# A mixture-of-experts stage with 96 instead of 128 slots for an expert, and up to three sweeps over the experts instead of two

## The chip, the core and the metric

The program runs on one NeuronCore of a Trainium2 chip. The core has five engines with programs of their own: TensorE (PE; matmuls, and PEld for its loads of the stationary operand), VectorE (DVE), ScalarE (ACT), GpSimd (POOL) and SyncE (SP), which issues most transfers. They wait for one another by semaphores. The metric is the device time of one execution in microseconds; of three runs of the kernel before, the median is 1677.79 us (1676.78 to 1679.43).

## The reference, cut to what matters

The trunk takes 256 frames of width 1024 through a retention layer with a dense SwiGLU, then a stick-breaking attention layer with a mixture of experts. All of it is float32. The change touches the last part alone:

```python
def moe_swiglu(h, router, w_in, w_out):
    hf = h.reshape(B * S, D)                       # 256 x 1024
    logits = (hf @ router).astype(jnp.float32)     # 8 experts
    top_v, top_i = lax.top_k(logits, TOP_K)        # 2 experts for each frame
    top_w = jax.nn.softmax(top_v, axis=-1)
    gates = jnp.sum(jax.nn.one_hot(top_i, N_EXPERTS) * top_w[..., None], axis=1)
    for e in range(N_EXPERTS):
        y = y + gates[:, e:e + 1] * swiglu(hf, w_in[e], w_out[e])
    # swiglu: a, b = split(h @ w_in); (silu(a) * b) @ w_out; w_in 1024 x 7168, w_out 3584 x 1024
```

256 frames with two choices each give 512 assignments for 8 experts, 64 on average.

## The kernel before, in words

**Precision.** A product of two float32 matrices is made from three passes (`passes`, L490 to L494): both operands are split into a high part, rounded to the type fp32r, and a low part, the rest; then high times high (L492), activations high times weights low (L493), and activations low times weights high (L494). The stationary operand (first argument) holds the activations, the moving one (second) 512 columns of weights.

**Weights.** They come in chunks of 1 MB into a ring of 6 raw slots, loaded by SP (L259, L270). A chunk is split in two quarters of 1024 columns each: ACT writes the high part (`w_hi`, L964), DVE the low part (`w_lo`, L1302), into rings of 3 slots. PE waits for DVE (`lo_done`), ACT waits for PE to free a slot (`w_used`), and SP waits for DVE to free a raw slot.

**Experts.** The router's choices become, for each expert, a list of slots: the first chosen frame takes slot 0, the next slot 1, and so on. `one_hot` (L1661) writes a matrix of frames by slots. `gather` (L869) multiplies it with the frames, so that an expert's frames stand in its slots; ACT copies the result (`ht`, L1230), PE transposes it in 8 blocks (`transpose_gathered`, L883), ACT and DVE split it in high and low (`hg_hi` L1234, `hg_lo` L1686). Then 7 tiles of 512 hidden columns follow. For one tile PE makes `up` twice (a and b, 24 matmuls each), ACT the silu (L1222), DVE the product with b (`e_g`, L1677), PE 4 transposes of it (`transpose_product`, L866), ACT and DVE its high and low part (`eT_hi` L1226, `eT_lo` L1681), and PE `down` (24 matmuls). `down` of a tile stands behind `up` of the next one on PE, so the split of its operand has a tile's time. `scatter` (L899, L900) brings the slots back to the frames, and DVE adds them with the gates (L1705). In a transpose the data is the stationary operand and the identity the moving one.

**Sweeps.** If the fullest expert has more frames than slots, the whole stage runs again for the frames left over (L1668: `npass` is 1 or 2), with the weights loaded again. Every engine reads `npass` and loops over it.

Of the kernel before, what the change touches and what calls it, by code (L numbers as in the profile page):

```python
# [16 lines left out]
P = 128  # L17
S = 256
D = 1024
NB = S // P  # L20
# [6 lines left out]
FW = 256  # L27
FT = FF // FW
NE, FE = 8, 3584
ET = FE // TW  # L30
EPS = 1e-6
RAW, RING = 6, 3
# [20 lines left out]
def trunk(nc, x_d, c_d, pos_d, ada_w, ada_b, norm_mix, norm_ff, ret_w_in, ret_gn, ret_w_out, kv_ada_w,  # L53
# [7 lines left out]
    with ctx:  # L61
# [105 lines left out]
            return buf.rearrange("p h (t q) -> p h t q", q=P)[:, :, 0:3:2, :]  # L167


        y32 = fa(0, D)  # L170
        e_sa = fa(2048, TW)
        e_g = fa(2560, TW)
        ht = fa(5120, D)
        hk_hi = hT_hi[:, :, :].rearrange("p c s -> p (c s)").rearrange("p (b d) -> p b d", b=NB)
        hk_lo = hT_lo[:, :, :].rearrange("p c s -> p (c s)").rearrange("p (b d) -> p b d", b=NB)
        hg_hi = ra(0, KC, P)
        hg_lo = ra(1024, KC, P)
        eT_hi = ra(2048, 4, P)
        eT_lo = ra(2560, 4, P)
        hot = ra(3072, NB, P)  # L180
        hotT = ra(3328, S)
        y_hi = ra(3584, D)
        y_lo = ra(4608, D)
# [55 lines left out]
        def _(sp):  # L239
# [249 lines left out]
        def _(pe):  # L489
# [367 lines left out]
            def down(c, m, n, first, last_one):  # L857

                pe.wait_ge(eTl_ok, n + 1)
                for h in range(2):  # L860
                    by_rows(c + h, m, eT_hi, eT_lo, 2 * h, 1, 4, first and h == 0, last_one and h == 1)

            def transpose_product(n):
                pe.wait_ge(eg_ok, n + 1)
                for c in range(4):
                    last = pe.transpose(ps[:, 2, c * P:(c + 1) * P], e_g[:, c * P:(c + 1) * P], ident[:, :])  # L866
                last.then_inc(eT_done, 1)

            def gather(ne):  # L869

                pe.wait_ge(hot_ok, ne + 1)
                for n in range(2):
                    cols = slice(n * TW, (n + 1) * TW)
                    for b in range(NB):
                        pe.matmul(ps[:, 6 + n, :], hot[:, b, :], hk_hi[:, b, cols], start=b == 0, stop=False)  # L875
                        last = pe.matmul(ps[:, 6 + n, :], hot[:, b, :], hk_lo[:, b, cols], start=False,  # L876
                                         stop=b == NB - 1)
                last.then_inc(ga_done, 1)

            def transpose_gathered(ne):  # L880
                pe.wait_ge(ht_ok, ne + 1)
                for c in range(KC):
                    last = pe.transpose(ps[:, 6 + c // 4, (c % 4) * P:(c % 4 + 1) * P], ht[:, c * P:(c + 1) * P],  # L883
                                        ident[:, :])
                last.then_inc(hgT_done, 1)

            def transpose_hot():
                for b in range(NB):
                    last = pe.transpose(ps[:, 3, b * P:(b + 1) * P], hot[:, b, :].bitcast(f32), ident[:, :])
                last.then_inc(hotT_done, 1)  # L890

            def scatter(ne):
# [29 lines left out]
            pe.wait_ge(hk_ok, 1)  # L922
            gather(0)
            pe.wait_ge(npass_ok, 1)
            npass = pe.value_load(npass_t[0:1, 0:1], min_val=1, max_val=2)
            with pe.Fori(0, npass) as p:
                m0 = NE * ET * p
                with pe.If(p):
# [23 lines left out]
        def _(act):  # L952
# [266 lines left out]
            def tile_silu(n, c, m):  # L1219

                act.wait_ge(w_used, before_half(c, m))
                act.activation(e_sa, ps[:, 0, :], ACT.Silu).then_inc(esa_ok, 1)  # L1222

            def tile_high(n):
                act.wait_ge(eT_done, n + 1)
                act.activation(eT_hi.rearrange("p c s -> p (c s)"), ps[:, 2, :], ACT.Copy).then_inc(eTh_ok, 1)  # L1226

            def gathered_out(ne):
                act.wait_ge(ga_done, ne + 1)
                act.activation(ht.rearrange("p (n q) -> p n q", n=2), ps[:, 6:8, :], ACT.Copy).then_inc(ht_ok, 1)  # L1230

            def gathered_high(ne):
                act.wait_ge(hgT_done, ne + 1)
                act.activation(hg_hi.rearrange("p (n c) s -> p n (c s)", n=2), ps[:, 6:8, :], ACT.Copy)\  # L1234
                   .then_inc(hgh_ok, 1)

            def y_high(ne):
# [3 lines left out]
            def step(j, me, ne, more=True):  # L1241

                c, n = U_MOE + 4 + RAW * (j - 1), me + j
                split_quarters(c, me, 5, 9)
                act.wait_ge(eg_ok, n)
                tile_silu(n, c + 2, me)
                split_quarters(c, me, 9, 12)
                if j < ET - 1 or more:
                    split_quarters(c, me, 12, 14)
                    if j == ET - 1:  # L1250
                        gathered_high(ne + 1)
                    split_quarters(c, me, 14, 17)
                tile_high(n)
                if j == ET:
                    y_high(ne)
                if j == 2:
                    act.wait_ge(hotT_done, ne + 1)
                    act.activation(hotT, ps[:, 3, 0:S], ACT.Copy).then_inc(hotT_ok, 1)
# [4 lines left out]
            npass = act.value_load(npass_t[0:1, 0:1], min_val=1, max_val=2)  # L1263
            with act.Fori(0, npass) as p:
                m0 = NE * ET * p
                with act.If(p):
# [26 lines left out]
        def _(dve):  # L1293
# [364 lines left out]
            def one_hot(ne, e):  # L1658

                for b in range(NB):  # L1660
                    ins = v.tensor_scalar(hot[:, b, :], slot_no[:, :], slot[:, b, ds(e, 1)], sel[:, b, ds(e, 1)],  # L1661
                                          ALU.is_equal, ALU.mult)
# [10 lines left out]
            def tile_product(n, c, m):  # L1673

                dve.wait_ge(esa_ok, n + 1)
                dve.wait_ge(w_used, before_half(c, m))
                v.tensor_tensor(e_g, ps[:, 1, :], e_sa, ALU.mult).then_inc(eg_ok, 1)  # L1677

            def tile_low(n):
                dve.wait_ge(eTh_ok, n + 1)  # L1680
                v.tensor_tensor(eT_lo.rearrange("p c s -> p (c s)"), ps[:, 2, :],  # L1681
                                eT_hi.rearrange("p c s -> p (c s)").bitcast(f32), ALU.subtract).then_inc(eTl_ok, 1)

            def gathered_low(ne):
                dve.wait_ge(hgh_ok, ne + 1)
                v.tensor_tensor(hg_lo.rearrange("p (n c) s -> p n (c s)", n=2), ps[:, 6:8, :],  # L1686
                                hg_hi.rearrange("p (n c) s -> p n (c s)", n=2).bitcast(f32),
                                ALU.subtract).then_inc(hgl_ok, 1)

            def y_gated(ne, c, m):  # L1690

                dve.wait_ge(w_used, before_half(c, m))
                v.tensor_tensor(y32.rearrange("p (n q) -> p n q", n=2), ps[:, 4:6, :],
                                gate_f[:, :].rearrange("p (n q) -> p n q", n=2), ALU.mult).then_inc(yg_ok, 1)

            def y_low(ne):
                dve.wait_ge(yh_ok, ne + 1)
# [33 lines left out]
                    one_hot(ne + 1, e + 1)  # L1731

            dve.wait_ge(npass_ok, 1)
            npass = dve.value_load(npass_t[0:1, 0:1], min_val=1, max_val=2)
            dve.wait_ge(gbc_ev, 4)
            with dve.Fori(0, npass) as p:
                steps.enter(p, 1)
# [92 lines left out]
```

## Time and profile before

| | |
|---|---|
| median of three runs | 1677.79 us |
| profiled execution, first to last instruction | 1675.8 us, 22,428 instructions |
| PE busy | 1565.9 us (93%), 7164 matmuls |
| PEld busy | 1294.4 us (77%) |
| DVE busy | 1405.6 us (84%) |
| ACT busy | 1085.8 us (65%) |
| HBM read | 499.28 MB, 299 GB/s over the span |
| granted TensorE clock | 0.968 of 2.4 GHz on average |

The page gives no time of the profiled execution but its span; the median of the runs lies 2.0 us above it. The stage of the experts goes from about 668 us to about 1667 us. A PE that is busy all the time is not a PE at its peak: matmuls overlap, each is recorded as some 0.39 us long, while they start 0.23 us apart.

### The profile page before, as it was taken

What the parts mean: (1) busy time and instruction counts of PE and PEld (TensorE: products, weight loads), DVE (VectorE), ACT (ScalarE), POOL (GpSimd) and SP (SyncE); (2) the same over time, 40 slices, a digit from 0 to 9 for tenths busy, and PEclk for the clock granted to TensorE, in tenths of its full rate; (3) what the DMA queues carried; (4) which work ended last, traced back from release to release, by engine and by line L of the source; (5) the groups of instructions that cost most, each with busy time, mean ns of one, the idle gap of its engine ahead of it and who ended that gap; (6) DMA issues with size and microseconds to landing.
All of it is one profiled execution on the core that took longest, in us unless ns stands there. A gap on an engine that the chain in (4) does not pass through costs nothing.

```text
span 1675.8 us, 22428 instructions
## 1 busy us (share of the span) xinstructions
PE 1565.9 (93%) x7164; PEld 1294.4 (77%) x7164; DVE 1405.6 (84%) x1537; ACT 1085.8 (65%) x1176; POOL 58.1 (3%) x47
## 2 busy tenths in 40 slices
PE   4999997999979676899999999999999999999996
PEld 4788775888768555788888888888888888888884
DVE  6889997788876444698998998998998998998995
ACT  3444434444454653687787777787787787787874
POOL 0212200000000120000000000000000000000000
PEclk9999998999989787899999999999999999999998
DMA  9977785888848102599999999999999999999991
GB/s 335 349 246 278 265 274 199 276 300 314 294 171 274 50 3 75 212 392 356 349 375 355 348 381 352 350 380 344 364 372 343 358 384 343 358 377 345 353 383 79
DMA packets 235113, 500.89 MB, mean 299 GB/s; under 512 B 9744, under 2 KB 40640, under 8 KB 235072
## 3 DMA queue, kind: packets, MB, share of 16 engines
q1 hardware_dynamic: 233904, 500.29, 82.6%
q8 instruction: 24, 0.39, 0.1%
q10 hardware_dynamic: 1168, 0.07, 0.0%
q14 instruction: 17, 0.14, 0.0%
HBM read 499.28 MB, written 1.05 MB: 299 GB/s over the span
## 4 chain that ended last, share of the span: by engine, by line
PE 81%; DVE 9%; DMA 3%; issue 3%; ACT 3%; POOL 1%; DVEq 0%; SPq 0%; ACTq 0%; POOLq 0%
PE ps L492 24%; PE ps L494 24%; PE ps L493 24%; DVE acc L1321 2%; DVE w_lo L1302 2%; DMA ada<-in_ada_w 2%; PE ps L866 1%; PE ps L767 1%; DMA raw<-in_ret_w_in 1%; PE ps L525 1%; DMA ada<-in_kv_ada_w 1%; PE ps L899 1%; PE ps L875 1%; PE ps L876 0%; PE ps L900 0%
## 5 line engine op out<-in xcount | busy, mean ns | idle before, releaser
L1302 DVE TENSOR_TENSOR w_lo<-raw,w_hi 128x1024 fp32r<-128x1024 f32 x834 | 990.9, 1225 | 100.2 <-ACT w_hi L964 86.2
L964 ACT ACTIVATE w_hi<-raw 128x1024 fp32r<-128x1024 f32 x834 | 864.5, 1058 | 246.3 <-PE ps L494 229.4
L492 PE MATMUL ps<-w_hi,RA 128*128 128x512 f32 x1560 | 618.1, 396 | 9.0 <-DVE w_lo L1302 2.9
L494 PE MATMUL ps<-w_hi,RA 128*128 128x512 f32 x1560 | 609.4, 391 | 0.0
L493 PE MATMUL ps<-w_lo,RA 128*128 128x512 f32 x1560 | 608.4, 390 | 0.0
L492 PEld LDWEIGHTS ps<-w_hi,RA 128*128 128x128 f32 x1560 | 293.7, 188 | 68.7 <-issue 3.4
L494 PEld LDWEIGHTS ps<-w_hi,RA 128*128 128x128 f32 x1560 | 293.4, 188 | 62.4
L493 PEld LDWEIGHTS ps<-w_lo,RA 128*128 128x128 f32 x1560 | 294.0, 188 | 59.4 <-issue 0.7
L492 PE MATMUL ps<-w_hi,hT_hi 128*128 128x512 f32 x432 | 172.6, 399 | 8.1 <-DVE hT_lo L1372 6.9
L494 PE MATMUL ps<-w_hi,hT_lo 128*128 128x512 f32 x432 | 170.2, 394 | 0.0
L493 PE MATMUL ps<-w_lo,hT_hi 128*128 128x512 f32 x432 | 170.1, 394 | 0.0
L1321 DVE SCALAR_TENSOR_TENSOR acc<-ada,cond,acc 128x512 f32<-128x512 f32 x189 | 150.6, 797 | 2.5
L492 PEld LDWEIGHTS ps<-w_hi,hT_hi 128*128 128x128 f32 x432 | 82.6, 191 | 25.7 <-DVE hT_lo L1372 7.7
L494 PEld LDWEIGHTS ps<-w_hi,hT_lo 128*128 128x128 f32 x432 | 82.2, 190 | 17.7
L493 PEld LDWEIGHTS ps<-w_lo,hT_hi 128*128 128x128 f32 x432 | 82.5, 191 | 16.6
L1226 ACT ACTIVATE RA<-ps 128x512 fp32r<-128x512 f32 x56 | 33.6, 600 | 61.6 <-PE ps L866 61.6
L1681 DVE TENSOR_TENSOR RA<-ps,RA 128x512 fp32r<-128x512 f32 x56 | 38.6, 689 | 22.8 <-ACT RA L1226 19.2
L1318 DVE TENSOR_SCALAR acc<-ada,cond 128x512 f32<-128x512 f32 x27 | 13.1, 484 | 36.9 <-DMA ada<-in_ada_w 34.5
L1222 ACT ACTIVATE FA<-ps 128x512 f32<-128x512 f32 x56 | 33.4, 596 | 13.8 <-PE ps L494 13.8
L1677 DVE TENSOR_TENSOR FA<-ps,FA 128x512 f32<-128x512 f32 x56 | 38.4, 685 | 3.1 <-PE ps L494 3.1
L525 PE MATMUL ps<-ident,FA 128*128 128x128 f32 x64 | 14.6, 422 | 27.6 <-DVE FA L1354 27.6
L1103 ACT ACTIVATE FA<-ps 128x512 f32<-128x512 f32 x11 | 6.6, 600 | 47.3 <-PE ps L494 47.3
(220 smaller groups left out, 874.0 us busy)
## 6 DMA issues: line engine op xcount, KB each, us to landing
raw<-in_moe_w_in SPq DMA_DIRECT2D x224, 1024.0 KB
raw<-in_moe_w_out SPq DMA_DIRECT2D x112, 1024.0 KB
ada<-in_ada_w SPq DMA_DIRECT2D x46, 1024.0 KB, 7.3
raw<-in_ff_w_in SPq DMA_DIRECT2D x44, 512.0 KB
raw<-in_ret_w_in SPq DMA_DIRECT2D x16, 1024.0 KB
raw<-in_ff_w_out SPq DMA_DIRECT2D x11, 1024.0 KB
raw<-in_ret_w_in SPq DMA_DIRECT2D x16, 512.0 KB
raw<-in_ret_w_out SPq DMA_DIRECT2D x8, 1024.0 KB
```

The source lines that it names most:

```text
L492: pe.matmul(out, a_hi, b_hi, start=first, stop=False)
L493: pe.matmul(out, a_hi, b_lo, start=False, stop=False)
L494: return pe.matmul(out, a_lo, b_hi, start=False, stop=last)
L525: last = pe.transpose(ps[:, c // 2, (c % 2) * S + b * P:(c % 2) * S + (b + 1) * P], (xn0 if n == 0 else xn)[:, b, c * P:(c + 1) * P], iden ...
L767: pe.matmul(o[:, 0:S], after[:, :], lm[:, h, 0:S], start=True, stop=False)
L964: act.activation(w_hi[:, cn % RING, cols], raw[:, cn % RAW, cols], ACT.Copy).then_inc(hi_done, 1)
L1222: act.activation(e_sa, ps[:, 0, :], ACT.Silu).then_inc(esa_ok, 1)
L1226: act.activation(eT_hi.rearrange("p c s -> p (c s)"), ps[:, 2, :], ACT.Copy).then_inc(eTh_ok, 1)
L1302: v.tensor_tensor(w_lo[:, cn % RING, cols], raw[:, cn % RAW, cols], w_hi[:, cn % RING, cols].bitcast(f32), ALU.subtract).then_inc(lo_done, 1)
L1321: ins = v.scalar_tensor_tensor(a, ada[:, h, cols], cond[:, kc:kc + 1], a, ALU.mult, ALU.add)
L1677: v.tensor_tensor(e_g, ps[:, 1, :], e_sa, ALU.mult).then_inc(eg_ok, 1)
L1681: v.tensor_tensor(eT_lo.rearrange("p c s -> p (c s)"), ps[:, 2, :], eT_hi.rearrange("p c s -> p (c s)").bitcast(f32), ALU.subtract).then_i ...
```

## The change

An expert gets `CAP = 96` slots. Everything with one column or one row for a slot shrinks with it: the one-hot matrix, the gathered frames, their transposes, the stationary operands of `up` and `down`, the transposes of the product, and the high and low parts of all these. Results of `up`, `down` and `gather` take 96 partitions in place of 128; their moving operand stays 512 columns wide. Tiles that have the slots on their partitions (`y32`, `e_sa`, `e_g`, `ht`, `hotT`, `y_hi`, `y_lo`) keep their row length. `down` has its own loop now, with the same order as `by_rows`. `npass` can be 1, 2 or 3, and takes one more DVE instruction; SP loops over the sweeps behind the first.

```diff
+CAP, SWEEPS = 96, 3
-        hg_hi = ra(0, KC, P)
+        hg_hi = ra(0, KC, CAP)
-        eT_hi = ra(2048, 4, P)
+        eT_hi = ra(2048, 4, CAP)
-            npass = sp.value_load(npass_t[0:1, 0:1], min_val=1, max_val=2)
+            npass = sp.value_load(npass_t[0:1, 0:1], min_val=1, max_val=SWEEPS)
             with sp.If(npass - 1):
-                experts(NE * ET)
+                with sp.Fori(1, npass) as p:
+                    experts(NE * ET * p)
-                        last = passes(ps[:, bank, :], hg_hi[:, kc, :], hg_lo[:, kc, :], w_hi[:, s, cols],
+                        last = passes(ps[0:CAP, bank, :], hg_hi[:, kc, :], hg_lo[:, kc, :], w_hi[:, s, cols],
...
-                    last = pe.transpose(ps[:, 2, c * P:(c + 1) * P], e_g[:, c * P:(c + 1) * P], ident[:, :])
+                    last = pe.transpose(ps[:, 2, c * CAP:(c + 1) * CAP], e_g[:, c * P:(c + 1) * P],
+                                        ident[0:CAP, 0:CAP])
...
-                    last = pe.transpose(ps[:, 6 + c // 4, (c % 4) * P:(c % 4 + 1) * P], ht[:, c * P:(c + 1) * P],
-                                        ident[:, :])
+                    last = pe.transpose(ps[:, 6 + c // 4, (c % 4) * CAP:(c % 4 + 1) * CAP], ht[:, c * P:(c + 1) * P],
+                                        ident[0:CAP, 0:CAP])
...
-                act.activation(eT_hi.rearrange("p c s -> p (c s)"), ps[:, 2, :], ACT.Copy).then_inc(eTh_ok, 1)
+                act.activation(eT_hi.rearrange("p c s -> p (c s)"), ps[:, 2, 0:4 * CAP], ACT.Copy).then_inc(eTh_ok, 1)
...
-            v.tensor_scalar(npass_t[:, :], stat[:, 16:17], float(P), 1.0, ALU.is_gt, ALU.add).then_inc(npass_ok, 1)
+            steps.link(v.tensor_scalar(stat[:, 20:21], stat[:, 16:17], float(CAP), 1.0, ALU.is_gt, ALU.add))
+            v.scalar_tensor_tensor(npass_t[:, :], stat[:, 16:17], float(2 * CAP), stat[:, 20:21], ALU.is_gt,
+                                   ALU.add).then_inc(npass_ok, 1)
...
-                v.tensor_tensor(eT_lo.rearrange("p c s -> p (c s)"), ps[:, 2, :],
+                v.tensor_tensor(eT_lo.rearrange("p c s -> p (c s)"), ps[:, 2, 0:4 * CAP],
...
-                steps.link(v.tensor_scalar(slot, slot, -float(P), None, ALU.add))
+                steps.link(v.tensor_scalar(slot, slot, -float(CAP), None, ALU.add))
```

No instruction changes its place; the forms change. On PE, at the end of a tile, before (partitions of the result by columns of the moving operand; `ident` with `FA` is a transpose, `w_hi` and `w_lo` with `RA` are the passes of `up` and `down`):

```order
L492 MATMUL ps<-w_hi,RA 128x512
L493 MATMUL ps<-w_lo,RA 128x512
L494 MATMUL ps<-w_hi,RA 128x512
L864 REGISTER_ALU
L866 MATMUL ps<-ident,FA 128x128 x4
L498 REGISTER_ALU
L492 MATMUL ps<-w_hi,RA 128x512
```

And the same place in the changed kernel:

```order
L494 MATMUL ps<-w_hi,RA 96x512
L495 MATMUL ps<-w_lo,RA 96x512
L496 MATMUL ps<-w_hi,RA 96x512
L874 REGISTER_ALU
L876 MATMUL ps<-ident,FA 128x96 x4
L500 REGISTER_ALU
L494 MATMUL ps<-w_hi,RA 96x512
```

The passes keep their 512 columns and write 96 partitions; the four transposes keep 128 partitions and have 96 columns. On DVE, ahead of the first tile, in the changed kernel (the slots, the one-hot matrix of the first expert, the count of the fullest expert and the number of sweeps):

```order
L1676 COPY FA<-ps 128x16
L1672 TENSOR_SCALAR RA<-slot_no,FA 128x96 x2
L1678 TENSOR_REDUCE stat<-ps 128x1
L1679 TENSOR_SCALAR stat<-stat 128x1
L1680 SCALAR_TENSOR_TENSOR npass_t<-stat 128x1
```

One instruction on 128x1 is added, L1679.

## Rows read from the trace of the kernel before

**Rows 1.** The page's 40 slices: granted TensorE clock, in tenths
```profile
PEclk9999998999989787899999999999999999999998
```

**Rows 2.** Stretches: length; PE, PEld, DVE, ACT, POOL busy us (count); clock, DMA share, GB/s
```profile
1109.63:1126.43 16.80, 16.80 (x79) 13.91 (x77) 15.45 (x15) 13.50 (x14) 0.00 (x0) 1.00 1.03 380
...
700.00:1640.00 940.00, 940.00 (x4285) 778.35 (x4284) 869.92 (x807) 747.05 (x785) 0.00 (x0) 1.00 0.99 362
```

**Rows 3.** Waits, 700 to 1640 us: total us, times, longest
```profile
ACT w_hi L964 <- PE ps L494: 119.8, 403, 0.7
ACT RA L1226 <- PE ps L866: 52.4, 54, 2.5
```

**Rows 4.** Groups by form, 700 to 1640 us: busy us, mean ns, idle before
```profile
L1302 DVE TENSOR_TENSOR w_lo<-raw,w_hi 128x1024 fp32r<-128x1024 f32 x650 | 765.5, 1221 | 49.1 <-ACT w_hi L964 35.8
...
L1681 DVE TENSOR_TENSOR RA<-ps,RA 128x512 fp32r<-128x512 f32 x54 | 37.2, 689 | 17.0 <-ACT RA L1226 13.4
...
L1226 ACT ACTIVATE RA<-ps 128x512 fp32r<-128x512 f32 x54 | 32.4, 600 | 52.4 <-PE ps L866 52.4
```

**Rows 5.** Timeline around one set of four transposes: start us, us long
```profile
1109.25 0.58 PEld L866 LDWEIGHTS ps<-ident,FA 128*128 128x128 f32 x4
1109.47 0.60 PE L866 MATMUL ps<-ident,FA 128*128 128x128 f32 x4
...
1109.80 0.19 PEld L492 LDWEIGHTS ps<-w_hi,RA 128*128 128x128 f32 x1
...
1109.91 0.19 PEld L493 LDWEIGHTS ps<-w_lo,RA 128*128 128x128 f32 x1
...
1110.14 0.39 PE L493 MATMUL ps<-w_lo,RA 128*128 128x512 f32 x1
```

**Rows 6.** Chain of waits, 1100 to 1140 us: start us, us on the chain
```profile
1109.63 0.44 PE ps L866 x4
...
1126.43 0.44 PE ps L866 x4
```

**Rows 7.** All transposes of the product, then of the gathered frames: ns min/median/max
```profile
L866 PE MATMUL ps<-ident,FA x224: 270/272/327, 691.5 to 1649.8; 128*128 128x128 f32 x112
...
L883 PE MATMUL ps<-ident,FA x64: 270/272/331, 673.4 to 1524.2; 128*128 128x128 f32 x64
```

**Rows 8.** Timeline of PEld alone: the first transpose load, then the first two merged
```profile
673.37 0.14 PEld L883 LDWEIGHTS ps<-ident,FA 128*128 128x128 f32 x1 [1.83 <-ACT FA L1230]
...
673.37 0.20 PEld L883 LDWEIGHTS ps<-ident,FA 128*128 128x128 f32 x2 [1.83 <-ACT FA L1230]
```

**Rows 9.** Timeline of PE in the retention layer: float32 without a split
```profile
120.52 0.60 PE L631 MATMUL ps<-FA 128*128 128x256 f32 x2
120.96 0.38 PE L632 MATMUL ps<-FA 128*128 128x128 f32 x2
121.18 0.60 PE L631 MATMUL ps<-FA 128*128 128x256 f32 x2
```

**Rows 10.** Timeline ahead of the first tile
```profile
667.76 0.60 DVE L1661 TENSOR_SCALAR RA<-slot_no,FA 128x128 fp32r<-128x128 f32 x2
...
673.37 1.09 PE L883 MATMUL ps<-ident,FA 128*128 128x128 f32 x8 [1.11 <-ACT FA L1230]
674.50 1.02 ACT L1234 ACTIVATE RA<-ps 128x1024 fp32r<-128x1024 f32 x1 [1.19 <-PE ps L883]
675.56 1.23 DVE L1686 TENSOR_TENSOR RA<-ps,RA 128x1024 fp32r<-128x1024 f32 x1 [4.67 <-ACT RA L1234]
...
676.93 0.79 PE L492 MATMUL ps<-w_hi,RA 128*128 128x512 f32 x1 [2.46 <-DVE RA L1686]
```

**Rows 11.** Timeline at the last tile
```profile
1650.08 0.60 ACT L1226 ACTIVATE RA<-ps 128x512 fp32r<-128x512 f32 x1 [7.54 <-PE ps L866]
1650.58 3.89 ACT L964 ACTIVATE w_hi<-raw 128x1024 fp32r<-128x1024 f32 x4
```

**Rows 12.** A load of 64 stationary columns in the attention, by form
```profile
L781 PEld LDWEIGHTS ps<-FA 128*64 128x64 f32 x16 | 1.2, 137 | 0.5
```

More of the change, by code:

```diff
@@ L167, in on_diagonal @@
             return buf.rearrange("p h (t q) -> p h t q", q=P)[:, :, 0:3:2, :]
[L170 to L173, printed above, removed]
+        y32 = fa(0, D)[0:CAP]
+        e_sa = fa(2048, TW)[0:CAP]
+        e_g = fa(2560, TW)[0:CAP]
+        ht = fa(5120, D)[0:CAP]
         hk_hi = hT_hi[:, :, :].rearrange("p c s -> p (c s)").rearrange("p (b d) -> p b d", b=NB)
         hk_lo = hT_lo[:, :, :].rearrange("p c s -> p (c s)").rearrange("p (b d) -> p b d", b=NB)
-        hg_hi = ra(0, KC, P)
-        hg_lo = ra(1024, KC, P)
-        eT_hi = ra(2048, 4, P)
[L179 to L183, printed above, removed]
+        hg_hi = ra(0, KC, CAP)
+        hg_lo = ra(1024, KC, CAP)
+        eT_hi = ra(2048, 4, CAP)
+        eT_lo = ra(2560, 4, CAP)
+        hot = ra(3072, NB, CAP)
+        hotT = ra(3328, S)[0:CAP]
+        y_hi = ra(3584, D)[0:CAP]
+        y_lo = ra(4608, D)[0:CAP]
         logit, gate_e, sel, slot, oh1, oh2, mx = (fa(3072 + 16 * n, NB, NE) for n in range(7))
@@ L860, in down @@
                 for h in range(2):
-                    by_rows(c + h, m, eT_hi, eT_lo, 2 * h, 1, 4, first and h == 0, last_one and h == 1)
+                    s = (c + h) % RING
+                    for t in range(2):
+                        landed(c + h, m, t)
+                        for k in range(2):
+                            cols = slice(t * D + k * TW, t * D + (k + 1) * TW)
+                            last = passes(ps[0:CAP, 4 + k, :], eT_hi[:, 2 * h + t, :], eT_lo[:, 2 * h + t, :],
+                                          w_hi[:, s, cols], w_lo[:, s, cols], first and h == 0 and t == 0,
+                                          last_one and h == 1 and t == 1)
+                        last.then_inc(w_used, 1)
             def transpose_product(n):
@@ L874, in gather @@
                     for b in range(NB):
-                        pe.matmul(ps[:, 6 + n, :], hot[:, b, :], hk_hi[:, b, cols], start=b == 0, stop=False)
-                        last = pe.matmul(ps[:, 6 + n, :], hot[:, b, :], hk_lo[:, b, cols], start=False,
+                        pe.matmul(ps[0:CAP, 6 + n, :], hot[:, b, :], hk_hi[:, b, cols], start=b == 0, stop=False)
+                        last = pe.matmul(ps[0:CAP, 6 + n, :], hot[:, b, :], hk_lo[:, b, cols], start=False,
                                          stop=b == NB - 1)
@@ L888, in transpose_hot @@
                 for b in range(NB):
-                    last = pe.transpose(ps[:, 3, b * P:(b + 1) * P], hot[:, b, :].bitcast(f32), ident[:, :])
+                    last = pe.transpose(ps[0:CAP, 3, b * P:(b + 1) * P], hot[:, b, :].bitcast(f32), ident[:, :])
                 last.then_inc(hotT_done, 1)
@@ L924, in _ @@
             pe.wait_ge(npass_ok, 1)
-            npass = pe.value_load(npass_t[0:1, 0:1], min_val=1, max_val=2)
+            npass = pe.value_load(npass_t[0:1, 0:1], min_val=1, max_val=SWEEPS)
             with pe.Fori(0, npass) as p:
@@ L1221, in tile_silu @@
                 act.wait_ge(w_used, before_half(c, m))
-                act.activation(e_sa, ps[:, 0, :], ACT.Silu).then_inc(esa_ok, 1)
+                act.activation(e_sa, ps[0:CAP, 0, :], ACT.Silu).then_inc(esa_ok, 1)
             def tile_high(n):
                 act.wait_ge(eT_done, n + 1)
-                act.activation(eT_hi.rearrange("p c s -> p (c s)"), ps[:, 2, :], ACT.Copy).then_inc(eTh_ok, 1)
+                act.activation(eT_hi.rearrange("p c s -> p (c s)"), ps[:, 2, 0:4 * CAP], ACT.Copy).then_inc(eTh_ok, 1)
             def gathered_out(ne):
                 act.wait_ge(ga_done, ne + 1)
-                act.activation(ht.rearrange("p (n q) -> p n q", n=2), ps[:, 6:8, :], ACT.Copy).then_inc(ht_ok, 1)
+                act.activation(ht.rearrange("p (n q) -> p n q", n=2), ps[0:CAP, 6:8, :], ACT.Copy).then_inc(ht_ok, 1)
             def gathered_high(ne):
                 act.wait_ge(hgT_done, ne + 1)
-                act.activation(hg_hi.rearrange("p (n c) s -> p n (c s)", n=2), ps[:, 6:8, :], ACT.Copy)\
+                act.activation(hg_hi.rearrange("p (n c) s -> p n (c s)", n=2), ps[:, 6:8, 0:4 * CAP], ACT.Copy)\
                    .then_inc(hgh_ok, 1)
@@ L1257, in step @@
                     act.wait_ge(hotT_done, ne + 1)
-                    act.activation(hotT, ps[:, 3, 0:S], ACT.Copy).then_inc(hotT_ok, 1)
+                    act.activation(hotT, ps[0:CAP, 3, 0:S], ACT.Copy).then_inc(hotT_ok, 1)
                 if j == ET - 2 and more:
@@ L1262, in _ @@
             act.wait_ge(npass_ok, 1)
-            npass = act.value_load(npass_t[0:1, 0:1], min_val=1, max_val=2)
+            npass = act.value_load(npass_t[0:1, 0:1], min_val=1, max_val=SWEEPS)
             with act.Fori(0, npass) as p:
@@ L1660, in one_hot @@
                 for b in range(NB):
-                    ins = v.tensor_scalar(hot[:, b, :], slot_no[:, :], slot[:, b, ds(e, 1)], sel[:, b, ds(e, 1)],
+                    ins = v.tensor_scalar(hot[:, b, :], slot_no[:, 0:CAP], slot[:, b, ds(e, 1)], sel[:, b, ds(e, 1)],
                                           ALU.is_equal, ALU.mult)
@@ L1676, in tile_product @@
                 dve.wait_ge(w_used, before_half(c, m))
-                v.tensor_tensor(e_g, ps[:, 1, :], e_sa, ALU.mult).then_inc(eg_ok, 1)
+                v.tensor_tensor(e_g, ps[0:CAP, 1, :], e_sa, ALU.mult).then_inc(eg_ok, 1)
             def tile_low(n):
                 dve.wait_ge(eTh_ok, n + 1)
-                v.tensor_tensor(eT_lo.rearrange("p c s -> p (c s)"), ps[:, 2, :],
+                v.tensor_tensor(eT_lo.rearrange("p c s -> p (c s)"), ps[:, 2, 0:4 * CAP],
                                 eT_hi.rearrange("p c s -> p (c s)").bitcast(f32), ALU.subtract).then_inc(eTl_ok, 1)
@@ L1685, in gathered_low @@
                 dve.wait_ge(hgh_ok, ne + 1)
-                v.tensor_tensor(hg_lo.rearrange("p (n c) s -> p n (c s)", n=2), ps[:, 6:8, :],
+                v.tensor_tensor(hg_lo.rearrange("p (n c) s -> p n (c s)", n=2), ps[:, 6:8, 0:4 * CAP],
                                 hg_hi.rearrange("p (n c) s -> p n (c s)", n=2).bitcast(f32),
@@ L1692, in y_gated @@
                 dve.wait_ge(w_used, before_half(c, m))
-                v.tensor_tensor(y32.rearrange("p (n q) -> p n q", n=2), ps[:, 4:6, :],
-                                gate_f[:, :].rearrange("p (n q) -> p n q", n=2), ALU.mult).then_inc(yg_ok, 1)
+                v.tensor_tensor(y32.rearrange("p (n q) -> p n q", n=2), ps[0:CAP, 4:6, :],
+                                gate_f[0:CAP, :].rearrange("p (n q) -> p n q", n=2), ALU.mult).then_inc(yg_ok, 1)
             def y_low(ne):
@@ L1733, in _ @@
             dve.wait_ge(npass_ok, 1)
-            npass = dve.value_load(npass_t[0:1, 0:1], min_val=1, max_val=2)
+            npass = dve.value_load(npass_t[0:1, 0:1], min_val=1, max_val=SWEEPS)
             dve.wait_ge(gbc_ev, 4)
```

## The prediction

> **What bounds the kernel now.** I read the page's slices first, then the stretch of the experts' tiles alone, its waits, and last the timeline of one tile's end. The slices show where the time lies: from slice 17 on, nearly all of it is the experts [rows 1]. In 940 us of that stretch PE is busy for 940.00 us at the full clock (1.00, that is 2.4 GHz); DVE is busy for 869.92 us (93%), ACT for 747.05 us, and the transfers take 0.99 of their engines at 362 GB/s [rows 2]. The waits say who is late: ACT's long sum of waiting is for PE, 119.8 us for a free weight slot and 52.4 us for the transposes [rows 3]. DVE's idle time before `w_lo` ends mostly by ACT [rows 4], which itself waits for PE. Nobody on PE waits for a weight, so PE's own instructions set the end here, and a change is worth what it takes off PE, as long as DVE (7% to spare) and the transfers keep up.
>
> One tile takes 1126.43 - 1109.63 = 16.80 us, of which the four transposes stand on the chain with 0.44 us [rows 6]. The other 72 matmuls share 16.36 us: 0.227 us each.
>
> **The 72 matmuls of a tile.** Their number and their 512 moving columns stay. What shrinks is the load of the stationary operand, 128 columns to 96. That load is covered: the next one follows a load after 0.11 us where nothing else holds it (1109.80 to 1109.91), while matmuls are 0.227 us apart [rows 5]. So I take nothing for it. The price bounds are these: 512 columns at 2.4 GHz are 0.213 us, so 0.014 us of each spacing is not streaming; if the load caused all of it and 96 columns removed it, 4032 + 64 of `gather` = 4096 matmuls would give 57 us. If a quarter went with a quarter of the columns, 14 us. The nearest row is the float32 matmul without a split: 256 columns, each held twice as long, with the same load of 128 columns, two of them in 120.96 - 120.52 = 0.44 us, 0.22 us each [rows 9]. There the load costs nearly nothing beyond streaming, so the excess seems to belong to how fp32r streams, and I stay at zero.
>
> **The transposes.** Here the moving operand is the identity, and it goes from 128 to 96 columns, while the stationary operand keeps 128. Which of the two sets their spacing? Four take 0.44 us, 0.109 us each [rows 6]. The float32 matmuls of 128 columns take the same: two in 121.18 - 120.96 = 0.22 us, and doubling the columns doubles the time [rows 9], so this spacing looks like 128 columns at two array clocks each (0.107 us). The load of a transpose is shorter: the first is 0.14 us long and the first two together 0.20 us, so the second began 0.06 us behind the first [rows 8], against 0.11 us between the loads for the passes. With 0.06 us of load under 0.107 us of streaming, the streaming sets the pace, and 96 columns take 0.080 us: 0.0267 us less for each.
>
> The Trainium skill, "TensorE: Matmul & The Clock Gate", section LDWEIGHTS, says the contrary for this case: a load costs its columns divided by 1.2 GHz, whatever the rows, and 128 columns would be 107 ns, just what is measured between transposes; the 128 columns stay, so by it nothing is gained. The 0.06 us between two such loads [rows 8] speaks against it. It is a rival below.
>
> Counts: 224 transposes of the product and 64 of gathered frames [rows 7], 288 in all; 288 x 0.0267 = 7.7 us. All 224 lie on PE's full stretch; of the 64, 8 are ahead of the first tile on the chain too [rows 10]. Each set's last transpose gives its share only if the load for the following pass, 0.11 us now [rows 5], shrinks with its columns. The load of 64 columns is 137 ns long [rows 12] against 0.19 us for 128 [rows 5], so it does; if it didn't, 64 sets would lose 1.7 us. I take 7.7 us.
>
> The two transposes of the one-hot matrix keep 128 moving columns; `scatter` keeps its 512 moving and 128 stationary columns: nothing.
>
> **Ahead of the first tile** the steps are one behind the other [rows 10]. ACT's copy costs 0.80 ns a column (1.02 us here for 1024, 0.600 for 512 [rows 4]): 256 columns less are 0.21 us. DVE's is 1.23 us here for 1024 and 0.689 for 512 [rows 4], 1.05 ns a column: 0.27 us. The one-hot matrix, two times 32 columns less: about 0.05 us. The added DVE instruction for the number of sweeps stands behind `one_hot`, which frees `gather`; PE's `gather` and ACT's copy of its result follow until the transposes start at 673.37 [rows 10], so it is hidden; without that cover it would be about 0.2 us (one small link of that chain). Sum 0.5 us. The clock changes level in this place (digits 7 and 8 in slices 15 and 16, counted from 0 [rows 1]), and a start 0.5 us earlier can shift one such level by a step; I allow 2 us for that either way.
>
> **In the tiles** ACT's `eT_hi` gets 128 x 0.80 = 0.10 us shorter and DVE's `eT_lo` 128 x 1.05 = 0.13 us; the hidden side of a pair, so they give only slack: DVE falls by 7 us of 870. **At the last tile** PE has no `up` to cover it: ACT starts `w_hi` only behind `eT_hi` [rows 11], so 0.10 us comes off the end.
>
> Register instructions and loop overhead on SP and PE stay as they are in the one sweep that runs. That only one runs follows from the reference itself: worked through on its own inputs, the fullest expert has 77 of the 512 assignments, and 76 to 86 with five other random draws. Transfers: the same bytes in 7.7 us less need 0.8% more than 362 GB/s; the tile looked at above ran at 380 GB/s [rows 2], so they follow.
>
> **Sum.** 7.7 + 0.5 + 0.1 = 8.3 us off the span of 1675.8 us, that is 1667.5 us. The median of the runs shown lies 2.0 us above the span, so 1677.8 - 8.3 = 1669.5 us.
>
> **The rivals.**
> - *The loads set the transposes' pace* (the 128 stationary columns stay). For it: the number 0.107 fits as well, and PEld is busy at the transposes without a gap [rows 5]. Against: the 0.06 us of [rows 8]. Then only 0.6 us is gained: 1677.2 us. The transfers could have the same outcome if the 0.99 share [rows 2] were a real ceiling, but then PE should wait for weights now and then.
> - *The passes get faster too.* For it: 0.014 us over streaming in each. Against: [rows 9]. By a quarter: 1669.5 - 14 = 1655.5 us. In full: 1669.5 - 57 = 1612 us on paper, but DVE has 7% and the transfers little more, so rather 1625 us.
> - *The load of 96 columns turns slow* and is no longer covered: the side that ends slower. The place is every pass; it decides only when a load takes over 0.227 us where it now takes 0.11. At four times the present rate for each column, 0.75 x 0.44 = 0.33 us, the spacing becomes 0.33 and 4096 x 0.10 = 420 us are added: about 2090 us. For it speaks no row; against it, the 64-column load of 137 ns [rows 12], which shows no cliff off the full width. The Trainium skill, same page, section on the weight-path modes, has a rule of this kind: fast loading needs exactly 128 weights and a type other than FP32. If the passes used it, 96 columns would lose it. Their load is no faster than one of plain float32 in this trace, so I see nothing to lose.
> - *A second sweep runs after all* (an expert with over 96 frames). It would double the stretch from 673 to 1667 us: some 2670 us. Only if the routing on the chip were far from the reference's.
>
> **How the numbers follow.** Transposes faster, passes unchanged: 60%, with its own range 1665 to 1675 us. Transposes unchanged or the gain lost to transfers: 17%. Passes faster as well: 18%, 10 of it for the small form. Loads slow: 4%. Second sweep: 1%. The predicted time is the first one's, 1669.5 us. The range takes in the second and the small form of the third and leaves out the rest: 1653 to 1679 us. What can be told from no change is about 0.2%, 3.4 us. Faster by more than that: the third case and nearly all of the first (8.3 us is well over 3.4, the shift of the clock may eat it in one of fifteen): 0.74. The same: the second case and the rest of the first: 0.20. Slower: 0.06, with a little for what I have not thought of.
>
> **What would show it.** Right: in the profile after, a set of four transposes on the chain takes about 0.33 us in place of 0.44, a tile 16.69 in place of 16.80 us, with PE still busy throughout and passes 0.227 us apart. The transposes' step is wrong if the set stays at 0.44. The step on the passes is wrong if their spacing falls below 0.225 or rises, and the cover is wrong if PE begins to wait for `w_lo`. A count of 7164 matmuls confirms one sweep.

## The result, and the profile after

The changed kernel takes 1687.0 us in the median of 5 runs (1686.36 to 1689.1), the kernel before 1679.43 us (5 runs, 1676.78 to 1682.88) beside it. The ratio is 1.0052 with a 95% interval of 1.0041 to 1.0063: 8.7 us slower by the ratio, 7.6 us by the two medians. Forecast were 8.3 us less, and a range of 1653 to 1679 us.

The profiled execution has a span of 1687.4 us, the slowest of its five runs (1684.6 to 1687.4). It has the same 7164 matmuls and HBM read the same 499.28 MB: one sweep ran. The stretch of the experts, in the columns of [rows 2], with one tile first:

```profile
1114.55:1131.60 17.05, 17.05 (x80) 11.97 (x78) 15.40 (x15) 13.44 (x14) 0.00 (x0) 1.00 1.01 376
...
700.00:1640.00 940.00, 940.00 (x4241) 661.97 (x4240) 855.34 (x799) 734.25 (x776) 0.00 (x0) 1.00 0.98 358
```

PE is still busy all the time at the full clock, so it is still what sets the end, and it gets through 4241 matmuls in 940 us where it was 4285. Every other engine has less to do: PEld 662 us against 778, DVE 855 against 870, ACT 734 against 747. The chain of waits around two sets of transposes, as in [rows 6]:

```profile
1114.56 0.33 PE ps L876 x4
1131.57 0.33 PE ps L876 x4
```

A set takes 0.33 us and not 0.44, as forecast. But the tile takes 1131.57 - 1114.56 = 17.01 us and not 16.80 [rows 6], so the 72 passes share 16.68 us: 0.2317 us each, where they had 0.2272. The timeline at that set answers to [rows 5]:

```profile
1114.17 0.39 PE L496 MATMUL ps<-w_hi,RA 128*96 128x512 f32 x1
1114.17 0.54 PEld L876 LDWEIGHTS ps<-ident,FA 96*128 96x128 f32 x4
...
1114.40 0.49 PE L876 MATMUL ps<-ident,FA 96*128 96x96 f32 x4
1114.65 0.16 PEld L494 LDWEIGHTS ps<-w_hi,RA 128*96 128x96 f32 x1
...
1114.73 0.17 PEld L495 LDWEIGHTS ps<-w_lo,RA 128*96 128x96 f32 x1
```

The load got shorter, 0.16 us where it was 0.19, and the next one follows after 0.08 us and not 0.11. It is covered with room to spare, and still the pass beside it became slower. Groups of the same stretch, the columns of [rows 4]:

```profile
L494 PE MATMUL ps<-w_hi,RA 128*96 128x512 f32 x1281 | 508.1, 397 | 0.0
L496 PE MATMUL ps<-w_hi,RA 128*96 128x512 f32 x1282 | 506.1, 395 | 0.0
...
L1694 DVE TENSOR_TENSOR RA<-ps,RA 128x384 fp32r<-128x384 f32 x53 | 29.4, 554 | 12.4 <-ACT RA L1237 12.4
...
L1237 ACT ACTIVATE RA<-ps 128x384 fp32r<-128x384 f32 x53 | 26.1, 493 | 47.9 <-PE ps L876 47.9
```

DVE's and ACT's part of the product got shorter as worked out (689 to 554 ns, 600 to 493 ns). PE waits for nobody at its passes (0.0).

The starts of successive passes show how the pace differs. Before, 89% of them are 226 or 227 ns, one behind the other; only the first nine behind a set of transposes are uneven (227 to 235 ns on average, single ones up to 236), and then the even step is found again. After, the passes of `up` and `down` never find it: of all steps 0.3% are 226 or 227 ns, 13% are at most 228, nearly half are over 231 and 16% are 236 or more. The mean between 700 and 1640 us (steps under 240 ns) is 227.2 ns before and 231.6 ns after.

**The account.** 4160 passes of the stage (4032 of `up` and `down`, 64 of `gather`, 64 of `scatter`) x 4.34 ns = 18.1 us more; transposes 7.7 us less; the short copies 0.6 us less: 9.8 us. The runs say 8.7 us (0.52%, 6.9 to 10.6 us). In the profiled executions the part from the first pass of `up` to the last set of transposes went from 972.5 to 981.3 us, 8.8 us, but the clock had a share in it: at its start PE ran at a granted clock of 0.50 (1.2 GHz) for 5.47 us before, and the same length was granted 0.73 on average after. The rows, in the columns of [rows 2], before and then after:

```profile
676.93:682.40 5.47, 5.47 (x13) 4.36 (x14) 1.23 (x1) 1.06 (x1) 0.00 (x0) 0.50 0.00 0
...
678.66:684.13 5.47, 5.47 (x18) 3.82 (x19) 1.23 (x1) 2.13 (x3) 0.00 (x0) 0.73 0.00 0
```

(0.73 - 0.50) x 5.47 = 1.3 us of full-speed work came free, so at one clock that part would have lost about 10.1 us; its share of the account is 10.6 us, because the copies and the first expert's transposes lie ahead of it. The spans of the two profiled executions differ by 11.6 us. Of this, 2.5 us arise ahead of the experts, where the code is the same, 0.8 us are won back ahead of the first tile, and 1.1 us come behind the last set of transposes, where the clock was lower (last section).

### The profile page after: what moved, and what is told of

It is laid out like the page before. It is cut to its first block, busy times and chain, and to the rows that moved or that the text cites. A ratio compares the mean times of both kernels' runs of the same rounds, so it can differ in the third digit from the quotient of the medians.

```text
span 1687.4 us, 22429 instructions
## 1 busy us (share of the span) xinstructions
PE 1573.7 (93%) x7164; PEld 1177.4 (70%) x7164; DVE 1399.8 (83%) x1538; ACT 1080.0 (64%) x1176; POOL 58.5 (3%) x47
## 3 DMA queue, kind: packets, MB, share of 16 engines
HBM read 499.28 MB, written 1.05 MB: 297 GB/s over the span
## 4 chain that ended last, share of the span: by engine, by line
PE 82%; DVE 8%; ACT 3%; issue 3%; DMA 2%; POOL 1%; DVEq 0%; SPq 0%; ACTq 0%; POOLq 0%
PE ps L494 25%; PE ps L496 25%; PE ps L495 25%; DVE w_lo L1313 2%; DVE acc L1332 2%; DMA ada<-in_ada_w 1%; PE ps L876 1%; PE ps L769 1%; DMA raw<-in_ret_w_in 1%; PE ps L527 1%; PE ps L886 1%; PE ps L887 0%; PE ps L910 0%; PE ps L911 0%; DVE FA L1487 0%
## 5 line engine op out<-in xcount | busy, mean ns | idle before, releaser
L494 PE MATMUL ps<-w_hi,RA 128*96 128x512 f32 (+1 forms) x1560 | 622.1, 399 | 8.4 <-DVE w_lo L1313 2.8
L496 PE MATMUL ps<-w_hi,RA 128*96 128x512 f32 (+1 forms) x1560 | 616.7, 395 | 0.0
L495 PE MATMUL ps<-w_lo,RA 128*96 128x512 f32 (+1 forms) x1560 | 613.1, 393 | 0.0
L494 PEld LDWEIGHTS ps<-w_hi,RA 128*96 128x96 f32 (+1 forms) x1560 | 258.4, 166 | 106.2 <-DVE w_lo L1313 3.0
L496 PEld LDWEIGHTS ps<-w_hi,RA 128*96 128x96 f32 (+1 forms) x1560 | 258.0, 165 | 103.7
L495 PEld LDWEIGHTS ps<-w_lo,RA 128*96 128x96 f32 (+1 forms) x1560 | 259.1, 166 | 99.9 <-issue 0.7
L495 PEld LDWEIGHTS ps<-w_lo,hT_hi 128*128 128x128 f32 x432 | 82.7, 191 | 16.7
L1237 ACT ACTIVATE RA<-ps 128x384 fp32r<-128x384 f32 x56 | 27.6, 493 | 57.8 <-PE ps L876 57.8
L1694 DVE TENSOR_TENSOR RA<-ps,RA 128x384 fp32r<-128x384 f32 x56 | 31.0, 554 | 18.1 <-ACT RA L1237 18.1
L1233 ACT ACTIVATE FA<-ps 96x512 f32<-96x512 f32 x56 | 33.2, 593 | 16.1 <-PE ps L496 16.1
L1690 DVE TENSOR_TENSOR FA<-ps,FA 96x512 f32<-96x512 f32 x56 | 38.0, 679 | 3.4 <-PE ps L496 3.4
L1114 ACT ACTIVATE FA<-ps 128x512 f32<-128x512 f32 x11 | 6.6, 598 | 47.3 <-PE ps L496 47.3
```

The source lines that it names most:

```text
L494: pe.matmul(out, a_hi, b_hi, start=first, stop=False)
L495: pe.matmul(out, a_hi, b_lo, start=False, stop=False)
L496: return pe.matmul(out, a_lo, b_hi, start=False, stop=last)
L1233: act.activation(e_sa, ps[0:CAP, 0, :], ACT.Silu).then_inc(esa_ok, 1)
L1690: v.tensor_tensor(e_g, ps[0:CAP, 1, :], e_sa, ALU.mult).then_inc(eg_ok, 1)
```

## The experiments

The theories: **A**, the number of loaded columns sets the passes' pace. **B**, the stride of 96 columns (384 bytes) between stationary blocks does. **C**, the shorter transposes or the 96 rows upset it. **F**, **G** and **H** came later and are told in place. "Spacing" is the mean step between starts of passes, 700 to 1640 us, steps under 240 ns. This limit is there to drop the steps over a set of transposes (285 ns and more); in the last row of the table it would also drop 166 steps of 240 and 241 ns within the series, so that row was taken with steps under 250 ns.

| kernel | spacing, ns | ratio to before (95%) |
|---|---|---|
| before | 227.2 | 1 |
| changed | 231.6 | 1.0052 (1.0041 to 1.0063) |
| full loads, 96 slots | 227.4 | 0.9972 (0.9960 to 0.9983) |
| 96-column loads, stride 128 | 230.0 | 1.0020 (1.0010 to 1.0029) |
| before, passes narrowed alone | 230.0 | 1.0066 (1.0050 to 1.0081) |
| full loads, 80 slots | 227.3 | 0.9952 (0.9939 to 0.9966) |
| stride 128, blocks in columns 32 to 127 | 231.6 | 1.0066 (1.0050 to 1.0082) |
| before, blocks moved by 32 columns | 232.9 | 1.0144 (1.0124 to 1.0163) |

**Full loads, short transposes.**

The diffs of this section show the lines that matter. Blocks of the other stationary operands (`hg_lo`, `eT_hi`, `eT_lo`, `hot`) are changed like `hg_hi`; where blocks are moved by 32 columns, the operands of `gather` and `scatter` move by 64.

```diff
-        hg_hi = ra(0, KC, CAP)
+        hg_hi = ra(0, KC, P)[:, :, 0:CAP]
...
+        hgw_hi, hgw_lo = ra(0, KC, P), ra(1024, KC, P)
...
-                        last = passes(ps[0:CAP, bank, :], hg_hi[:, kc, :], hg_lo[:, kc, :], w_hi[:, s, cols],
+                        last = passes(ps[:, bank, :], hgw_hi[:, kc, :], hgw_lo[:, kc, :], w_hi[:, s, cols],
```

> The changed kernel, but up, down and gather load all 128 stationary columns again (32 of them unused, blocks at a stride of 128 columns) and write 128 partitions; the transposes keep their 96 moving columns. Theory A (the number of loaded columns sets how evenly the passes follow one another): spacing back to 226 to 227 ns, time 7.7 us under before, about 1671.5. Theory B (the stride of 96 columns, 384 bytes, of the stationary blocks is to blame): the same. Theory C (the shorter transposes or the 96 rows upset the passes): spacing stays near 231 to 232 ns, time 1685 to 1690.

Measured: 1673.98 us against 1679.09 us for before; spacing 227.4 ns. The short transposes are still there, so they don't upset the passes, and this half of C falls. The other half stays open: the passes write 128 partitions again, so the width of the load and the rows written came back together. The chain around two sets of transposes:

```profile
1226.37 0.33 PE ps L879 x4
1243.09 0.33 PE ps L879 x4
```

A tile takes 16.72 us. The passes are back, and the transposes' gain is there, but not all of it: from the start of the last pass ahead of a set to the start of the second behind it, before takes 901 ns, the changed kernel 794 and this one 824. About one transpose's share (30 ns of 107) is missing. It went where the following load has 128 columns again, the case that the prediction had priced. A set of four gains 77 ns, and one of eight should gain seven shares, 187 ns. With 77 x 56 + 187 x 8 = 5.8 us for the transposes, 0.6 for the copies and 0.7 lost on the passes the sum is 5.7 us; measured are 0.28%, 4.7 us (2.9 to 6.7).

A part of the 0.7 us is in `scatter`. Its operands lie where they lay before, and it still loads 128 columns and streams 512, but it has 96 rows in place of 128. Its steps between 700 and 1640 us went from 226.7 ns to 229.6 (L913 to L914) and 231.7 ns (L914 to L913).

**Loads of 96 columns at a stride of 128.**

```diff
-        hg_hi = ra(0, KC, CAP)
+        hg_hi = ra(0, KC, P)[:, :, 0:CAP]
```

> The changed kernel with its 96-column loads, but the blocks of the stationary operands lie at a stride of 128 columns (512 bytes) as before. Theory A: nothing changes, spacing 231 to 232 ns, 1685 to 1690 us. Theory B: spacing back to 227 ns, about 1671.5 us. Theory C: as A.

Measured: 1682.06 us, spacing 230.0 ns. Neither theory alone: the stride is worth 1.5 ns of the 4.3, and 2.8 ns stay. 4160 x 2.8 ns = 11.6 us less the 8.3 us won are 3.3 us over before; the ratio says 3.4 us.

**The passes narrowed alone**, on the kernel before:

```diff
-                        last = passes(ps[:, bank, :], hg_hi[:, kc, :], hg_lo[:, kc, :], w_hi[:, s, cols],
+                        last = passes(ps[0:96, bank, :], hg_hi[:, kc, 0:96], hg_lo[:, kc, 0:96], w_hi[:, s, cols],
```

> The kernel before, with one part of the change alone: up and down load 96 of the 128 columns (stride 128) and write 96 partitions; gather and the transposes stay at 128 columns. Theory A: the loss without the gain, 4032 passes each 4 to 5 ns slower, 16 to 20 us over before, 1694 to 1700. Theory B or C: no change, 1677 to 1682.

Measured: 1690.9 us against 1679.09, 11.1 us more by the ratio; spacing 230.0 ns. 4032 x 2.8 ns = 11.3 us. The loss comes without the gain; it is smaller than A said, since the stride stayed. The chain shows the old sets and the new pace, (17.01 - 0.44) / 72 = 0.2301 us:

```profile
1118.11 0.44 PE ps L874 x4
1135.12 0.44 PE ps L874 x4
```

**The passes alone on an idle core.** A program of nothing but passes, one run of each, first for widths and strides. A load of fewer columns also writes fewer partitions in these programs:

> Leaves out the whole trunk: 216 passes in a row on an idle core, high and low operands as in the kernel, for each of these stationary widths (and strides): 128 (128), 96 (96), 96 (128), 128 (132), 112 (128), 64 (128), 120 (128), 32 (128), 80 (128), 128 (128), 96 (96). Theory A: 226 to 227 ns at 128 columns with either stride, 231 to 232 at 96 with either stride. Theory B: 226 to 227 at a stride of 128 whatever the width, more at 96 (96) and 128 (132). If the cause needs the other engines' traffic in SBUF, all are equal.

Rows of one line each: the first of the three passes of a series, its count, ns min/median/max, first and last start in us. Between the first and the last of 72 lie 213 steps.

```profile
L70 PE MATMUL ps<-w_hi,a_hi x72: 389/392/398, 69.5 to 118.9; 128*96 128x512 f32 x72
...
L77 PE MATMUL ps<-w_hi,a_hi x72: 390/392/393, 119.6 to 168.6; 128*96 128x512 f32 x72
...
L84 PE MATMUL ps<-w_hi,a_hi x72: 387/396/398, 169.3 to 218.7; 128*128 128x512 f32 x72
...
L126 PE MATMUL ps<-w_hi,a_hi x72: 389/389/393, 469.3 to 517.6; 128*128 128x512 f32 x72
```

In order: 96 columns at a stride of 96, (118.9 - 69.5) / 213 = 231.9 ns; 96 at 128, 230.0 ns; 128 at 132, 231.9 ns; 128 at 128, 226.8 ns. The kernels' values come back with no other engine at work, so neither transfers nor ACT and DVE are needed for it. The other widths, all at a stride of 128: 32 columns 231.6, 64 230.0, 80 233.3, 112 228.9, 120 233.3 ns. That is no function of the amount loaded: 120 columns are slower than 32, and 128 with an odd stride as slow as 96. A and B both fall as stated.

**Places.**

> Leaves out the whole trunk; passes in a row on an idle core as in the study of widths, 168 for each entry: width (stride, first column; moving columns and their shift; rows). 128 (128, 4), 128 (128, 16), 128 (128, 32), 128 (128, 64), 96 (128, 16), 96 (128, 32), 128 (0, 0), 96 (0, 0), 128 (128, 0; 512 shifted by 16), 128 (128, 0; 512 shifted by 64), 96 (128, 0; 512 shifted by 32), 128 (128, 0; 256), 96 (128, 0; 256), 128 (128, 0; 384), 96 (128, 0; 384), 128 (160, 0), 128 (128, 0; 512; 96 rows), 112 (112, 0), 96 (192, 0), 128 (128, 0). Theory A2 (the count of loaded columns alone): 226.8 ns wherever 128 are loaded, 230 wherever 96 are. Theory B2 (what matters is where both operands lie against each other in SBUF): 226.8 only where the blocks start at multiples of 128 columns, and 96 columns at 0 stride or other starts move too. Theory E (a step in time: the pace of loads and streams must match): 226.8 for 128 with a step of zero, and a change of the moving columns to 256 or 384 moves the excess over 0.4167 ns a column.

Full loads of 128 columns, in ns: first column 0 or 64, 226.8; 4, 233.8; 16, 233.3; 32, 232.4; stride 160, 231.8; stride 0, 226.7; moving operand shifted by 16, 229.0, by 64, 226.8. With 96 rows in place of 128: 226.7, so rows alone did not upset this series, other than in `scatter` above. 112 columns at a stride of 112: 232.3. Loads of 96 columns: at 0, 230.0 with a stride of 0, 128 or 192, and 231.7 with the moving operand shifted by 32; at 16, 228.3; at 32, 226.7. The last one writes 96 partitions at the even pace, so writing fewer partitions is not by itself what costs.

Fewer moving columns: with 256, 120.0 ns for 128 stationary columns and 116.0 for 96; with 384, 173.3 and 175.0; with 512, 226.8 and 230.0. With 128 columns the excess over streaming (256 / 2.4 = 106.7, 384 / 2.4 = 160.0, 512 / 2.4 = 213.3) is about 13.3 ns whatever the length of the stream; a column costs (226.7 - 120.0) / 256 = 0.417 ns, one clock at 2.4 GHz. With 96 columns it is 9.3, 15.0 and 16.7 ns: the narrower load wins 4 ns in the short stream and loses 3 in the long one. So the size and even the sign of the effect hang on the length of the stream. The two series with 256 moving columns, (463.4 - 443.6) / 165 and (482.9 - 463.8) / 165:

```profile
L140 PE MATMUL ps<-w_hi,a_hi x56: 276/283/283, 443.6 to 463.4; 128*128 128x256 f32 x56
...
L147 PE MATMUL ps<-w_hi,a_hi x56: 274/278/282, 463.8 to 482.9; 128*96 128x256 f32 x56
```

The 226.7 ns of 96 columns at 32 gave theory **F**: what counts is whether the last column ends at a multiple of 64. Two kernels and one more program tested it:

```diff
-        hg_hi = ra(0, KC, CAP)
+        hg_hi = ra(0, KC, P)[:, :, P - CAP:P]
```

> The changed kernel with loads of 96 columns, all its short forms and a stride of 128 columns, but each stationary block lies in columns 32 to 127 of its 128 in place of 0 to 95, so that it ends at a multiple of 64 columns (256 bytes). Theory F (what counts is where the last loaded column lies in SBUF, modulo 64 columns; the width only moves it): spacing 226 to 227 ns, and the gain that was forecast, 7.7 + 0.6 us, 1669 to 1671.5 us. Theory A (width): 230 ns as with the blocks at 0 to 95, 1681 to 1685 us.

Measured: 1689.7 us against 1678.67, spacing 231.6 ns. F falls. The other one is before with

```diff
-        hg_hi = ra(0, KC, P)
+        hg_hi = ra(32, KC, P)
```

> The kernel before with all its 128-column loads and 128-column transposes; only the places of up's and down's stationary blocks move by 32 columns (128 bytes), and gather's and scatter's operands by 64. No instruction changes its form. Theory F: the passes of up and down go from 227 to about 232.4 ns, 4032 x 5.4 = 22 us more, 1700 us. Theory A: no change, 1677 to 1680 us.

Measured: 1702.68 us against 1678.67, 24 us more, with no instruction changed in form; spacing 232.9 ns, and 4032 x 5.7 ns = 23 us. Its chain, (17.23 - 0.44) / 72 = 0.2332 us:

```profile
1120.43 0.44 PE ps L866 x4
1137.66 0.44 PE ps L866 x4
```

A place alone costs more than the whole change did.

> Leaves out the whole trunk; passes in a row on an idle core, 168 for each entry, width (stride, first column; moving columns, their shift): 96 (128, 32), 96 (128, 96), 64 (128, 64), 32 (128, 96), 112 (128, 16), 80 (128, 48), 120 (128, 8), 96 (96, 32), 128 (192, 0), 96 (128, 32; 256), 128 (128, 0; 256), 96 (128, 32; 384), 96 (128, 32; 512 shifted by 32), the same by 64, 128 (128, 0; 512 by 32), 128 (128, 32; 512 by 32), 128 (128, 4; 512 by 4), 64 (128, 0), 96 (128, 64), 96 (128, 0). Theory F: all that end at a multiple of 64 columns with the moving operand there too take 226 to 227 ns (the first seven, the ninth, shift 64); shifting the moving operand alone upsets it. Theory G (only the place of both against each other counts): 128 (128, 32; by 32) and 128 (128, 4; by 4) are at 226.8 again. Theory A: width alone, 226.8 for 128 and 230 or more for the rest.

```profile
L161 PE MATMUL ps<-w_hi,a_hi x56: 392/394/398, 515.9 to 554.4; 128*128 128x512 f32 x56
...
L168 PE MATMUL ps<-w_hi,a_hi x56: 389/389/397, 555.1 to 592.5; 128*128 128x512 f32 x56
```

The first has the moving operand shifted by 32 columns alone: (554.4 - 515.9) / 165 = 233.3 ns. The second has the stationary one shifted by 32 too: 226.7 ns. So the two places count against each other (theory **G**), at least for 32; shifting both by 4 gave 231.1 ns. 96 columns fit in: with both operands shifted by 32 they take 230.0 ns, as with both at 0, and they take 230.0 at 64 as well. But 96 columns at 32 with the moving operand at 0, which had been at 226.7, stood at 231.7 here. With 256 and 384 moving columns they took 120.0 and 173.3 ns, the values of 128 columns. The rest: 96 at 96, 231.6; 96 at 32 with a stride of 96, 231.8; 64 at 0, 230.1; 32 at 96, 230.7; 64 at 64, 230.0; 112 at 16, 231.7; 80 at 48, 231.1; 120 at 8, 226.7; 128 at a stride of 192, 226.7.

**History.**

> Leaves out the whole trunk; passes in a row on an idle core, 168 for each entry, all with 512 moving columns, width (stride, first column): 128 (128, 0), 96 (128, 32), 96 (128, 16), 96 (128, 32), 96 (128, 0), 96 (128, 32), 96 (96, 0), 96 (128, 32), 128 (128, 4), 128 (128, 0), 120 (128, 0), 120 (128, 8), 128 (128, 0), 120 (128, 8), 96 (128, 0), 120 (128, 8), 96 (96, 0), 128 (128, 0), 96 (128, 0), 96 (128, 16), 96 (128, 32). Theory H (a pattern can run at more than one pace, and what ran before it decides): 96 (128, 32) is at 226.7 ns behind 96 (128, 16) and at about 231.8 behind others, 120 (128, 8) too may differ, while 128 (128, 0) finds 226.8 behind anything and 96 (128, 0) stays at 230.0. Theory F or G (places alone decide): every entry with the same numbers has the same spacing.

```profile
L70 PE MATMUL ps<-w_hi,a_hi x56: 389/389/389, 57.8 to 95.2; 128*96 128x512 f32 x56
...
L98 PE MATMUL ps<-w_hi,a_hi x56: 389/394/398, 211.0 to 249.2; 128*96 128x512 f32 x56
...
L182 PE MATMUL ps<-w_hi,a_hi x56: 389/389/395, 674.2 to 711.6; 128*128 128x512 f32 x56
```

The first two are the same series, 96 columns at 32. Behind full loads of 128 it runs at (95.2 - 57.8) / 165 = 226.7 ns, behind 96 at 0 at (249.2 - 211.0) / 165 = 231.5 ns (231.7 from unrounded starts), and stays there for all its 168 passes. Theory **H** holds: it has two paces. The last row is 128 columns at 0 behind the slow 96 (96): 226.7 ns, as behind everything that it was put behind. It is the pattern that found the even step from each state tried; 120 at 8 did so too, in three places here and one in the program before. 96 at 0 stays at 230.0 and 96 (96) at 231.9 in each of its places. H went wrong in one detail: behind 96 (128, 16) the series at 32 took 226.7 once and 231.6 once.

**80 slots.** Full loads and `CAP = 80`:

> The version with full loads of 128 columns and the short transposes, with 80 slots in place of 96 (the fullest expert has 77). If only the moving columns of the transposes count and each set gives back its last share to the load of 128 columns: 3 x 56 + 7 x 8 = 224 transposes, each 16 columns x 0.83 = 13.3 ns less than with 96, so 3.0 us under the version with 96 slots and full loads, 1671 us. If the passes are upset by the place of the blocks or by the transposes: slower than it.

Measured: 1670.44 us against 1677.49, ratio 0.9952; a set of transposes takes 0.28 us:

```profile
1104.94 0.28 PE ps L879 x4
1121.62 0.28 PE ps L879 x4
```

The step over a set of transposes takes 784 ns, 40 less than with 96 slots: three shares of 13.3 ns, as worked out, so the transposes are paid by their moving columns. The ratios put it 3.4 us under the 96 slots, where 3.0 were worked out, but both intervals together leave some 3 us either way. It is the fastest version run, and it fits only while no expert gets over 80 frames; five other draws gave 76 to 86 for the fullest expert, and over 80 a second sweep over the experts comes. The version with 96 slots and full loads beats both kernels as well, at 0.9972.

## Why the prediction was wrong, by its steps

- **What bounds the kernel: right.** PE is busy for 940 of 940 us before and after, and what moved PE's pace moved the time.
- **The transposes, 0.0267 us for each: right.** The set on the chain went from 0.44 to 0.33 us, and the step over it from 901 to 794 ns, 107 ns as worked out. Their loads still have 128 columns, and they start 81 or 82 ns apart. By the rule of the Trainium skill ("TensorE: Matmul & The Clock Gate", section LDWEIGHTS) such a load takes 107 ns; the trace does not agree, and the rival that the prediction took from it falls.
- **"That load is covered ... So I take nothing for it": the step that failed.** The load is covered, and shrank; the pass still costs 4.3 ns more, 18 us in the sum where the prediction had put nothing. Its own sign of error came out: passes 0.227 us apart were forecast, and their spacing rose to 0.232 us. The bounds given for it, 0 to 57 us of gain, had no loss in them: the excess of 0.014 us over streaming was taken as a cost that a smaller load could only lessen. The trace had a sign of it that was not read: the nine uneven steps (227 to 235 ns on average) behind each set of transposes, with the very same forms, show that the even 226.8 ns is a state that can be lost. The prediction took the means of a tile and of float32 matmuls and never looked at single steps.
- **The rival on the slower side named the right place and the wrong mechanism.** It asked that a load outlast 0.227 us. A load of 96 columns takes 161 ns, where one of 128 took 188. The slowdown came with a load that was faster.
- **Ahead of the first tile and at the last one: right in kind.** ACT's `hg_hi` takes 0.81 us (1.02), DVE's `hg_lo` 0.96 us (1.23), the pair 0.48 us less. From the one-hot matrix to the first pass of `up` it is 8.39 us (9.17).
- **One sweep, and transfers that follow: right**, though the latter was never put to the test.

Open stays why the places matter. Shown are these: giving the passes their 128-column loads and 128 written partitions back brings the pace back; narrowing these alone loses it; the pace depends on where one operand lies against the other, on width and partitions written, on the length of the stream and on what ran before; other engines and transfers are not needed for it. Rows (the partitions read) had no part in the series on the idle core, but in `scatter` the pace changed with them, and no run tells why the two differ. What makes the steps even or uneven is not settled by these runs, nor could the width be told from the number of partitions written, which goes with it in every run. Nor does any theory here forecast the pace of a new place: F and A fell, G holds for shifts of 32 and not of 4, and H says only that the past counts.

## What to carry to other kernels

A covered load is not a free parameter: before narrowing or packing a stationary operand, look at the steps between starts of successive matmuls. If they are all alike, the stream is in an even state that a change of width, stride or offset can lose; here blocks of 128 columns that start at multiples of 64 columns, with the moving operand at multiples of 64 too, kept it. Unused columns in them cost nothing in the passes, and one transpose's share (30 ns) at the end of each set. For streams of 512 columns of this type: narrow what is streamed (the identity of a transpose), leave what is loaded. With 256 columns the narrower load was no slower, so measure at the length that you have.

## What the runs showed of the hardware that was not expected

- The same 168 passes at the same addresses ran at 226.7 or at 231.6 ns, depending on what had run before, and kept it to the end of the series.
- The last 24 passes of `down` stand behind about 3 us of idle PE. They took 5.73 us in the profiled run of before (granted clock 1.00), 7.36 us in that of the changed kernel (0.77) and 8.54 us with full loads and 96 slots (0.65). So up to 2.8 us between two profiled executions hang on the clock; with one profile of each kernel it isn't shown whether that is chance or the kernel:

```profile
1644.90:1653.50 8.60, 8.54 (x24) 6.48 (x24) 3.38 (x3) 1.56 (x2) 0.00 (x0) 0.65 0.00 0
```

This row is of full loads and 96 slots, in the columns of [rows 2]. That version's profiled run gained 6.2 us from the first pass of `up` to the last set of transposes (972.5 to 966.3 us), of which 1.3 us are the clock again (0.74 against 0.50 in its first 5.47 us), and what follows gave 2.3 us back.
